# A transformer trunk's opening: x and the second weight slab issued behind a wait, the third slab split ahead of the first gate

## What is computed

```
rms_norm(x, g) = x * rsqrt(mean(x * x) + 1e-6) * g
swiglu_ffn(x, w_in, w_out) = (silu(gate) * up) @ w_out     with  gate, up = split(x @ w_in, 2)
x = x + 0.5 * swiglu_ffn(rms_norm(x, ffn1_norm), ffn1_w_in, ffn1_w_out)
x = x + mixer(rms_norm(x, mix_norm))
x = x + 0.5 * swiglu_ffn(rms_norm(x, ffn2_norm), ffn2_w_in, ffn2_w_out)
```

## Time and profile before

| what | before |
|---|---|
| median of 3 runs | 888.23 us |
| the profiled execution, its own time | 888.76 us |
| its span in the trace | 887.0 us |
| TensorE busy (PE) | 879.4 us, 99% |
| weight load busy (PEld) | 733.9 us, 83% |
| VectorE busy (DVE) | 565.2 us, 64% |
| ScalarE busy (ACT) | 422.0 us, 48% |
| GpSimd busy (POOL) | 78.1 us, 9% |
| moved by DMA | 181.74 MB, mean 205 GB/s |

### The profile page before, as it was taken

The page is one execution under the profiler, slowest core; times in us unless marked ns, Lnnn a source line. Parts: engine busy times, 40 slices in busy tenths (PEclk is TensorE's granted clock), DMA queues, the critical chain, the costliest instruction groups (busy, mean ns, idle before and its releaser), DMA issues.

```text
span 887.0 us, 11328 instructions
## 1 busy us (share of the span) xinstructions
PE 879.4 (99%) x4102; PEld 733.9 (83%) x4102; DVE 565.2 (64%) x598; ACT 422.0 (48%) x471; POOL 78.1 (9%) x70
## 2 busy tenths in 40 slices
PE   9999999999999999999999999999999999999997
PEld 7888888889888888888888888888899888888886
DVE  5875565758967756556477556555687666655643
ACT  7644443548845634344345444343663445434432
POOL 1000000428820000000020000000300000000000
PEclk9999999999999999999999999999999999999999
DMA  8987567555254875776729756746575368675722
GB/s 285 289 267 241 190 205 250 161 178 195 68 189 134 294 236 181 242 246 212 242 84 296 249 193 213 239 168 210 187 285 168 118 195 271 220 238 164 238 73 83
DMA packets 152812, 181.74 MB, mean 205 GB/s; under 512 B 8205, under 2 KB 137257, under 8 KB 152776
## 3 DMA queue, kind: packets, MB, share of 16 engines
q1 hardware_dynamic: 152184, 180.72, 62.5%
q10 hardware_dynamic: 592, 0.53, 0.2%
HBM read 168.11 MB, written 1.05 MB: 191 GB/s over the span
## 4 chain that ended last, share of the span: by engine, by line
PE 98%; DMA 1%; DVE 1%; ACT 0%; SPq 0%; issue 0%; POOL 0%; POOLq 0%; DVEq 0%
PE ga L1321 11%; PE acc L1321 11%; PE ub L1321 10%; PE ub L1322 10%; PE ub L1323 10%; PE acc L1323 10%; PE acc L1322 10%; PE ga L1323 10%; PE ga L1322 10%; PE tp L1395 1%; PE ga L1591 1%; DMA raw<-in_ffn_w_in_dram 1%; PE tp L1678 0%; PE ub L1625 0%; PE tp L1604 0%; PE tp L1615 0%
## 5 line engine op out<-in xcount | busy, mean ns | idle before, releaser
L914 DVE TENSOR_TENSOR w_lo<-raw,w_hi 128x2048 fp32r<-128x2048 f32 x143 | 324.3, 2291 | 67.2 <-ACT w_hi L604 66.9
L604 ACT ACTIVATE w_hi<-raw 128x2048 fp32r<-128x2048 f32 x151 | 284.5, 1907 | 20.1 <-DMA raw<-in_ffn_w_in_dram 17.1
L1321 PE MATMUL acc<-w_hi,act_hi 128*128 128x512 f32 x416 | 163.2, 392 | 0.2 <-DVE act_lo L1258 0.2
L1323 PE MATMUL acc<-w_hi,act_lo 128*128 128x512 f32 x416 | 161.8, 389 | 0.0
L1322 PE MATMUL acc<-w_lo,act_hi 128*128 128x512 f32 x416 | 161.7, 389 | 0.0
L1321 PE MATMUL ga<-w_hi,xn_hi 128*128 128x512 f32 x384 | 150.8, 393 | 0.2 <-DVE w_lo L1022 0.2
L1323 PE MATMUL ga<-w_hi,xn_lo 128*128 128x512 f32 x384 | 149.6, 390 | 0.0
L1321 PE MATMUL ub<-w_hi,xn_hi 128*128 128x512 f32 x384 | 149.6, 390 | 0.0
L1322 PE MATMUL ga<-w_lo,xn_hi 128*128 128x512 f32 x384 | 149.5, 389 | 0.0
L1323 PE MATMUL ub<-w_hi,xn_lo 128*128 128x512 f32 x384 | 149.4, 389 | 0.0
L1322 PE MATMUL ub<-w_lo,xn_hi 128*128 128x512 f32 x384 | 149.4, 389 | 0.0
(11 more groups left out here) (170 smaller groups left out, 676.7 us busy)
## 6 DMA issues: line engine op xcount, KB each, us to landing
raw<-in_ffn_w_in_dram SPq DMA_DIRECT2D x172, 512.0 KB, 5.1
raw<-in_ffn_w_out_dram SPq DMA_DIRECT2D x88, 512.0 KB, 4.0
xs<-xs SPq DMA_DIRECT2D x176, 64.0 KB, 2.1
raw<-in_sgu_w_in_dram SPq DMA_DIRECT2D x16, 512.0 KB, 4.9
raw<-in_ab_w_in_dram SPq DMA_DIRECT2D x12, 512.0 KB, 5.1
raw<-in_ab_w_out_dram SPq DMA_DIRECT2D x8, 512.0 KB, 3.6
raw<-in_sgu_w_out_dram SPq DMA_DIRECT2D x8, 512.0 KB, 4.2
raw<-in_ffn_w_in_dram SPq DMA_DIRECT2D x8, 256.0 KB, 6.0
```

Source lines behind the costliest of these rows:

```text
L604: act.activation(w_hi[:, n % RING, :], raw[:, n % RAW, :], ACT.Copy).then_inc(hi_split, 1)
L914: dve.tensor_tensor(w_lo[:, n % RING, :], raw[:, n % RAW, :], w_hi[:, n % RING, :].bitcast(F32), ALU.subtract).then_inc(lo_split, 1)
L1321: pe.matmul(dst, s_hi, m_hi, start=start, stop=False)
L1323: return pe.matmul(dst, s_lo, m_hi, start=False, stop=stop)
```

## The change

SP waits, after the four quarters of slab 0, until the first two of them have landed, and issues the other three pieces of x and everything behind them only then. On ScalarE, the square of x (1, 0) moves from behind slab 0 to behind the second channel half of x's second token half, and the second piece of slab 2 moves ahead of the first gate. On VectorE, the second piece of slab 2 moves ahead of the first product.

```diff
@@ sync @@
                     if k == 0:
                         load_x(0, 0)
                         load_quarters(0, w_in, 0, pair(0, FF))
+                        sp.wait_ge(early_landed[0], 32)
                         load_x(1, 0)
                         load_x(0, 1)
                         load_x(1, 1)
@@ scalar, opening @@
                 piece(0, 1536, 2048, raw_landed[0])
-                square(1, 0)
                 pair_hi(1, 0)
                 pair_hi(1, 1)
                 second_hi(0)
                 piece(1, 0, 1024, early_landed[1])
                 piece(1, 1024, 2048, raw_landed[1])
                 second_hi(1)
+                square(1, 0)
                 square(0, 1)
                 piece(2, 0, 1024, raw_landed[2])
+                piece(2, 1024, 2048, raw_landed[2])
                 gate_rows(0, 0, 0, 0, ACT.Silu, scaled=True)
-                piece(2, 1024, 2048, raw_landed[2])
                 square(1, 1)
@@ vector, opening @@
                 mean_eps(0, 3)
                 piece(2, 0, 1024, 5)
+                piece(2, 1024, 2048, 3)
                 product_rows(0, 0, scaled=True)
                 to_blocks(0, 0)
-                piece(2, 1024, 2048, 3)
                 mean_eps(1, 4)
```

## The result

Slower: 889.75 us, the median of 22 runs (889.04 to 890.61), against 888.12 for 22 runs of the kernel before (887.51 to 888.88). The ratio is 1.0017, with a 95% interval of 1.0011 to 1.0023, or 1.0 to 2.0 us. The forecast was 888.4 us with a range of 887.8 to 889.2, so the result lies outside it.

What follows compares the result with a forecast made beforehand. TensorE, busy 99% of the span, was the bound. A new stop of +0.41 ahead of unit 1 and a removed one of -0.23 ahead of unit 2 made +0.18: 888.94 profiled, 888.4 us as median, range 887.8 to 889.2.

Steps and rivals of the forecast that it cites:

- Only the opening counts: TensorE's stops before unit 2, 0.24 at 10.29 and 0.23 at 31.90, together 0.47 us, are all that can be had.
- The first matmul does not move: TensorE's opening: the first real matmul stays at 7.92 because TensorE is still in its warm-ups.
- the first half of slab 0 is worth nothing: Opening: 0.57 us of earlier landing of this half would be absorbed by TensorE's warm-ups.
- x (1, 0) lands at 9.4, as before: SP queue: issued 2.8 us later, this load still lands when TensorE is ready; bounds 8.75 to 12.25.
- Rival C: Loads late at TensorE's transposes of x (1, 0), no slack: slower, 888.9 to 889.4, far end 891.2; chance 0.20.
- I put 0.1 us on every later landing: SP queue behind the wait: it hardly runs dry, so later loads land 0.1 us later, bounds -0.2 and +0.7.
- Does slab 0's second half land earlier when x is not behind it?: Opening loads: answered no, it lands at 8.8 either way; earlier would end a stop of 0.24 at 10.29.
- rival B: Slab 0's second half lands earlier and ScalarE's chain is shorter, so stops go, none comes: -0.47, 887.8; chance 0.15.
- The stop at 10.29: TensorE ahead of slab 0's third chunk: a stop of 0.16, 0.24 with restart, not forecast to end.
- The stop ahead of unit 1: TensorE, due at 20.87, waits for product_rows behind slab 2's second piece: new stop of 0.33, 0.41 with restart.
- The stop ahead of unit 2 goes: TensorE's stop at 31.90 ends because slab 5 is issued 0.7 us earlier: -0.23.
- Moving square(1, 0) costs nothing: ScalarE: slab 2's first piece starts at 17.15 instead of 16.89; its landing has 0.3 of slack.

Runs made afterwards that it cites:

- run 9: The changed kernel measured again for a second trace: 889.72 us, ratio 1.0017 to the kernel before.
- run 1: Kernel before plus only the wait on SP ahead of x, for the first half of slab 0: 888.79 us, ratio 1.0009.
- run 8: The whole change with square(1, 0) left at its old place: 889.28 us, ratio 1.0014 to the kernel before.
- run 11: The changed kernel with 14 warm-up products in place of 17: 889.98 us, ratio 1.0019 to the kernel before.
- run 2: Kernel before with only slab 2's second piece moved ahead of the first gate and product: 887.99 us, ratio 0.9999.
- run 3: Kernel before with only square(1, 0) moved behind second_hi(1): 888.79 us, ratio 1.0005.
- run 4: The whole change without the wait on SP: 888.42 us, ratio 1.0002 to the kernel before.
- run 10: Kernel before with 14 warm-up products in place of 17: 887.92 us, ratio 0.9997.
- run 12: Kernel before with slab 2 split first and 14 warm-up products, no wait, square(1, 0) at its old place: 887.88 us, ratio 0.9998.
- run 6: Kernel before with the wait for slab 0's first half placed behind x (1, 0), the first of three x pieces: 888.89 us, ratio 1.0008.

## Why the prediction was wrong, step by step

- **Only the opening counts: right.** In all fourteen profiled executions the run's time less the start of unit 2 is 856.5 to 856.9 us (before 888.76 - 31.90 = 856.86; after 889.40 - 32.74 = 856.66). The whole difference is made ahead of unit 2.
- **The first matmul does not move, and the first half of slab 0 is worth nothing: right in effect.** 8.00 and 8.03 after, 7.92 before. In part that is luck: between traces it moves by more than a microsecond with TensorE's rate (see the last section).
- **x (1, 0) lands at 9.4, as before: wrong, on the harmless side.** It was issued at 5.50 and landed 2.8 later, at 8.3. TensorE's transposes had no wait. Rival C, late loads, had the mechanism, a price a little low (888.9 to 889.4) and the wrong place: slab 1, not x (1, 0), was late.
- **The step that failed**: "The queue holds half of slab 0 when the wait passes, so it hardly runs dry [...] For that I put 0.1 us on every later landing (bounds -0.2 and +0.7)". It did run dry. When the wait passed, at 5.50, the trace of after had moved 1.11 MB of the 1.31 that x (0, 0) and slab 0 are, so about 0.2 MB stood in the queue and not the half slab of 0.52. At 350 GB/s that is an estimated 0.6 us of work, while the first piece of x landed 2.8 us after its issue. With the wait ahead of x, for the first half of slab 0, five traces have slab 1 landing at 14.5, 15.2, 14.1, 15.0 and 13.7 (after, and runs 9, 1, 8 and 11): 14.5 on average. Without a wait, six traces (before, and runs 2 to 4, 10 and 12) give 13.8, 13.3, 13.1, 12.7, 13.8 and 13.5: 13.4. The first half, which sets the stop, is later by as much: 13.0 on average against 11.9. The term is +1.1 and not +0.1, beyond the bound of +0.7. I had reasoned that the slowest engine still has work when the wait passes. But the others empty, and time is lost again behind it, in the second trough, for which I had no term at all.
- **"Does slab 0's second half land earlier when x is not behind it? In the forecast no": wrong, and worth nothing.** Its last quarter lands 4.3 to 4.8 us after its issue in the six traces with the wait ahead of x, against 4.9 to 6.0 in the six without a wait. So the argument against rival B, that x took nothing from slab 0, doesn't hold for all that stands behind slab 0. The stop at 10.29 went with it, but ScalarE and VectorE are ahead of TensorE there in most runs anyway, and the loss behind is larger.
- **One trace as the base.** The trace of before had slab 1 at 13.8, the latest of the six, and from its first matmul to the third chunk (7.92 to 10.29) it took 2.37, where the other five took 1.81 to 1.96. So that stop was of some 0.5 us and not of the 0.24 in the prediction, since TensorE's transposes were held up as well, and most of it was chance. Its stop ahead of unit 2 is in none of runs 2 to 4. Set against that trace, the change looks 0.64 long; the medians say 1.6.
- **The stop ahead of unit 1: right as a mechanism, too small in company.** Forecast 0.33; without the wait 0.27, with the wait 0.53 (and 0.52 in the second trace), since ScalarE's chain behind a late slab 1 has no slack and carries the moved square.
- **The stop ahead of unit 2 goes: right, for another reason.** Slab 5 was issued at 21.22 instead of 21.41, not 0.7 earlier, since all of VectorE's chain was late, and it reached ScalarE at 27.41, later than before. TensorE merely came later itself.
- **Moving square(1, 0) costs nothing: not settled.** Three pairs differ in its place alone (before and run 3, runs 2 and 4, run 8 and after). Their medians put 0.6, 0.4 and 0.5 us on it, each inside the intervals.
- The rule of the Trainium skill in "DMA: Bandwidth & Descriptors", "Rules for kernel authors", to issue early and wait late, pointed the right way. The runs add when: deferring slab 1 by 1.4 us didn't delay its landing with x in the queue; deferring x with it, so that the queue empties, did.

## What to carry to other kernels

A wait put on a transfer queue to favour what is in front can cost as soon as the queue empties before the next transfer's first packets. Reckon what will still stand in the queue when the wait passes, not when it is issued (here 0.2 MB of slab 0 were too little; with 0.75 MB of x besides, slab 1 landed on time), or leave the wait out. When what is at stake is a microsecond of 888, take several traces of the kernel before: a stop seen in one of them may be chance, and a landing time is a distribution. Compute moved to fill an idle slot may be free only while the transfer behind it is on time; cost it together with the transfer's delay, not beside it.

## What the runs showed of the hardware

- **A restarted queue runs thin a second time.** Behind the nearly empty stretch, from 8.2 to 10.4 us, only some 190 GB/s moved with transfers issued and waiting (188 and 189 in the traces of after and run 1, 205 to 249 in those of runs 8, 9 and 11), against 354 to 384 in the same stretch of the six traces without a wait. The packets themselves are slower there, 0.10 us each against 0.05. The kernel that waits for all of slab 0 shows it too, from 11. Why is open: the rate at which SP issues (a quarter of 0.25 MB every 0.5 us) would allow 500 GB/s. No run took it apart.
- **TensorE's rate rises at another moment in each run, and that is a likely part of the scatter.** The 24 warm-up records stand 0.21 apart at first and 0.11 later (in run 1 they are at 0.11 from the first), which fits the clock's two levels of 1.2 and 2.4 GHz; the granted clock of the profile says 1.00 throughout and does not show it. TensorE was busy without a gap in both of the traces below. Warm-ups in three stretches of 1 us, the kernel before and then the one with the wait behind x:

```profile
4.80:5.80 1.00, 0.95 (x5) 1.00 (x6) 1.00 0.92 310
5.80:6.80 1.00, 1.00 (x11) 1.00 (x11) 1.00 0.76 204
6.80:7.80 1.00, 1.00 (x12) 1.00 (x11) 1.00 0.86 290
```

```profile
4.80:5.80 1.00, 0.95 (x5) 1.00 (x6) 1.00 0.96 329
5.80:6.80 1.00, 1.00 (x7) 1.00 (x7) 1.00 0.71 231
6.80:7.80 1.00, 1.00 (x6) 1.00 (x6) 1.00 1.01 372
```

  The second one reached the higher rate two microseconds later, and its first matmul came at 8.89. Over the fourteen traces the first matmul came between 7.37 and 8.89, in the eleven with all warm-ups the later the later the rate rose; the runs of one kernel spread by as much, 1.4 us. A late first matmul also gives slab 1 more time: from 8.89 on, that kernel ran to unit 2 at 32.18 without a single stop.
- **A transfer lands later when more is issued behind it.** Slab 0's last quarter is issued at 2.76 in every kernel. It lands 4.9 to 6.0 us later in the six traces without a wait, and 4.3 to 4.8 in the six with the wait ahead of x. With the wait behind all of x, so that x is queued and slab 1 is not, it takes 4.8, and the quarter has 1.4 us from the landing of the first half (6.13 to 7.6), as with the wait ahead of x (1.3 to 1.8), where the kernels without a wait have 2.0 to 2.8. So it is slab 1's issue more than x's that comes with the delay, in one trace; in that of run 6, with only x (1, 0) queued, it takes 5.0. How it acts was not looked into.
- **The same load takes another time in each run.** Slab 1, issued from 4.7 in all six traces without a wait, landed between 12.7 and 13.8; slab 5's second half took 4.9 to 5.4 us from its issue in runs 2 to 4, and 7.1 in run 12.
